# Block 2's keys and values as two split units, compression in four column groups of the array, and these units in another order

## The reference

```python
h = rms_norm(x, norm_mix_g[i]);  proj = h @ w_in[i]
q_r, k_r, v_r, g_r, q_n, kv_n, gate_n, m_a, m_b = jnp.split(proj, cuts, axis=-1)
y_ret = (silu(g_r) * groupnorm(retention(rotary(q_r), rotary(k_r), v_r))) @ w_o_ret[i]
kv = kv_n.reshape(B, T, 6, NSA_KV_GROUPS, NSA_HD)      # k_c v_c k_s v_s k_w v_w, 2 groups of 64
kc = compress(k_c)  # blocks of 32 tokens, every 16: gelu((block + pos) flattened to 2048 @ w1) @ w2
vc = compress(v_c)
o_n = g0 * softmax(q kc) vc + g1 * softmax(q k_s) v_s + g2 * softmax(q k_w) v_w   # 16 heads of 64
y_nsa = o_n @ w_o_nsa[i]
x = x + (sigmoid(m_a) * y_ret + sigmoid(m_b) * y_nsa) @ w_out[i]
h = rms_norm(x, norm_ffn_g[i]);  a, b = split(h @ w_ffn_in[i]);  x = x + (silu(a) * b) @ w_ffn_out[i]
```

## Time and profile before

| what | value |
|---|---|
| median of 3 runs | 2225.61 us (2225.45 to 2229.24) |
| the profiled execution | 2225.84 us |
| its span in the trace | 2224.0 us |
| TensorE busy | 2128.4 us, 96% of the span |
| TensorE weight loads busy | 1881.1 us, 85% |
| VectorE busy | 846.8 us, 38% |
| ScalarE busy | 1057.9 us, 48% |
| GpSimd busy | 1604.9 us, 72% |
| weights read | 336.83 MB |

### The profile page before, as it was taken

How to read it: one execution, slowest core, us unless ns; L and a number is a source line. 1 busy time by engine, 2 the same in 40 slices (tenths; PEclk the granted TensorE clock), 3 DMA queues, 4 the chain that set the end, 5 groups by cost and what they waited for, 6 DMA issues and landing times. The chain is left out here.

```text
span 2224.0 us, 33226 instructions
## 1 busy us (share of the span) xinstructions
PE 2128.4 (96%) x13056; PEld 1881.1 (85%) x13056; DVE 846.8 (38%) x1849; ACT 1057.9 (48%) x2037; POOL 1604.9 (72%) x1279
## 2 busy tenths in 40 slices
PE   7999999996999999999999999999999999999998
PEld 6788999795878999897687888998987777889996
DVE  3432464166532465091402182331433220553221
ACT  3344565443244565444452475444454522665443
POOL 6295898892386898898892508988997844348887
PEclk9899999997999999999999999999999998999999
DMA  7644455451044575545345404554554445225553
GB/s 246 130 157 146 152 190 190 174 201 38 1 151 152 163 232 191 201 161 180 114 180 186 152 1 152 178 176 178 183 180 149 152 155 173 76 69 165 185 190 123
DMA packets 217696, 343.17 MB, mean 154 GB/s; under 512 B 8611, under 2 KB 124419, under 8 KB 217413
## 3 DMA queue, kind: packets, MB, share of 16 engines
q1 hardware_dynamic: 205688, 331.35, 43.3%
q10 hardware_dynamic: 11853, 9.70, 2.3%
HBM read 336.83 MB, written 4.19 MB: 153 GB/s over the span
## 5 line engine op out<-in xcount | busy, mean ns | idle before, releaser
L1354 POOL TENSOR_TENSOR w_lo<-ring,w_hi 128x512 fp32r<-128x512 f32 x1184 | 1544.8, 1322 | 519.8 <-ACT w_hi L1460 466.6
L1460 ACT ACTIVATE w_hi<-ring 128x512 fp32r<-128x512 f32 x1184 | 742.7, 633 | 839.2 <-PE bank L701 338.3
L701 PE MATMUL bank<-x_hi,w_hi 128*128 128x256 f32 x2080 | 593.9, 286 | 13.9 <-POOL w_lo L1354 13.6
L704 PE MATMUL bank<-x_lo,w_hi 128*128 128x256 f32 x2080 | 591.0, 284 | 0.0
L705 PE MATMUL bank<-x_hi,w_lo 128*128 128x256 f32 x2080 | 590.9, 284 | 0.0
L701 PEld LDWEIGHTS bank<-x_hi,w_hi 128*128 128x128 f32 x2080 | 401.8, 193 | 17.2 <-issue 9.9
L704 PEld LDWEIGHTS bank<-x_lo,w_hi 128*128 128x128 f32 x2080 | 402.0, 193 | 0.2
L705 PEld LDWEIGHTS bank<-x_hi,w_lo 128*128 128x128 f32 x2080 | 401.7, 193 | 0.0
L726 PE MATMUL bank<-w_hi,x_hi 128*128 128x512 f32 x720 | 292.7, 407 | 20.0 <-POOL w_lo L1354 16.5
L729 PE MATMUL bank<-w_lo,x_hi 128*128 128x512 f32 x720 | 283.9, 394 | 0.0
L730 PE MATMUL bank<-w_hi,x_lo 128*128 128x512 f32 x720 | 283.7, 394 | 0.0
(11 more groups left out here) (314 smaller groups left out, 2396.4 us busy)
## 6 DMA issues: line engine op xcount, KB each, us to landing
ring<-in_w_in SPq DMA_DIRECT2D x72, 1024.0 KB, 6.7
ring<-in_ffn_w_up SPq DMA_DIRECT2D x44, 1024.0 KB, 7.6
ring<-in_w_ffn_in SPq DMA_DIRECT2D x44, 1024.0 KB, 6.6
ring<-in_ffn_w_down SPq DMA_DIRECT2D x20, 1024.0 KB, 6.0
ring<-in_w_ffn_out SPq DMA_DIRECT2D x20, 1024.0 KB, 6.3
ring<-in_xattn_wkv SPq DMA_DIRECT2D x16, 1024.0 KB, 6.3
ring<-in_w_o_ret SPq DMA_DIRECT2D x16, 1024.0 KB, 6.0
ring<-in_od_w_in SPq DMA_DIRECT2D x12, 1024.0 KB, 7.0
```

Source lines behind the costliest of these rows:

```text
L701: m = mm(out_, view(w_hi)[:, k, :], x_hi[:, 4 * kh + k, :], start=start, stop=False)
L704: mm(out_, view(w_hi)[:, k, :], x_lo[:, 4 * kh + k, :], start=False, stop=False)
L1354: tt(view(w_lo), src, view(w_hi), ALU.subtract).then_inc(w_lo_ready, 1)
L1460: return A(o, i_, ACT.Copy, **kw)
```

## The change

The three units of keys and values become two split ones: `kk` (512 columns: the compression's keys and values, the selected keys, the window keys; by channels) and `vv` (304 columns: the selected and the window values and the gates; by tokens, with pieces of 304). Each loads two ranges of columns side by side into its slot. The order becomes `kk`, `qn0`, `cmp_k`, `qn1`, `cmp_v`, `mb0`, `vv`, `mb1`. The compression's 16 matmuls go in turn to four groups of 32 columns of the array, each with its own 32 partitions of bank 6; its four partial sums lie there one under the other, ACT copies them out, and one matmul with `c_fold` (four identity matrices of 32 one under the other) both adds and turns them; the Gelu then stands behind that. Turning the hidden layer and the product with the second matrix are put inside `mb0`, the scores with the compressed keys inside `vv`. The compressed values of two heads stand side by side, so L867's matmul serves two heads. VectorE zeroes the padded tensors in POOL's place, and `xnT` is no longer built in Block 2.

```diff
-            cols(units, f"{L}kv_a", w, KV_N, 384)
-            cols(units, f"{L}kv_b", w, KV_N + 384, 128)
-            cols(units, f"{L}kv_c", w, KV_N + 512, 304)
-            for j, n in enumerate("kv"):
...
+            two_ranges(f"{L}kk", 512, (0, KV_N, 384), (384, KV_N + 512, 128))
+            cols(units, f"{L}qn0", w, Q_N, 512)
+            compression("k")
+            cols(units, f"{L}qn1", w, Q_N + 512, 512)
+            compression("v")
+            cols(units, f"{L}mb0", w, M_B, 512)
+            two_ranges(f"{L}vv", VALUES, (0, KV_N + 384, 128), (128, KV_N + 640, 176))
+            cols(units, f"{L}mb1", w, M_B + 512, 512)
...
-                                    o_last=(a % 4 == 3 and b == 1), extra=a if b == 0 else None))
+                                    o_last=(a % 4 == 3 and b == 1), extra=a if a % 2 == 0 and b == 0 else None))
...
-                    mm(bank[b][:, c:c + SEQ], n_vc[:, a % 4, g, 64 - 64 * par:192 - 64 * par], n_pcT[:, a // 4, :],
-                       start=first, stop=False)
+                    mm(bank[b][:, c:c + SEQ], n_vc[:, a % 4 // 2, a // 8, :], n_pcT[:, a // 4, :], start=first, stop=False)
...
-                        m = mm(bank[6][0:2 * N_CMP, 0:256], n_x[j][:, lp, :], ring[:, s, lp * 256:(lp + 1) * 256],
-                               start=lp == 0, stop=lp == 15)
+                        part = 32 * (lp % 4)
+                        m = mm(bank[6][part:part + 32, 0:256], n_x[j][:, lp, :], ring[:, s, lp * 256:(lp + 1) * 256],
+                               start=lp < 4, stop=lp >= 12)
...
+                            m = mm(bank[7][:, (2 * j + c) * 32:(2 * j + c + 1) * 32], n_hid[j][:, c * P:(c + 1) * P], c_fold, start=True, stop=True)
...
+                hidden_units(0)
                 channel_major(f"{L}qn1", x_parts)
...
+                hidden_units(1)
+                token_major(f"{L}mb0", x_parts, second_half=turn_hidden, after=compressed)
+                token_major(f"{L}vv", x_parts, second_half=compressed_scores)
+                token_major(f"{L}mb1", x_parts)
...
-                for v in (n_ks, n_kw):
-                    nc.gpsimd.memset(v.rearrange("p a b -> p (a b)"), 0.0)
...
+                B.wait_full(dve, (f"{L}oret", 1, 1))
+                for v in (n_ks, n_kw):
+                    nc.vector.memset(v.rearrange("p a b -> p (a b)"), 0.0)
```

More of the change, by code:

```diff
@@ L353, in build @@
         rt_lo, rt_hi = parts[:, 0:16, :], parts[:, 16:32, :]
[L354 to L355 removed]
+        n_x = [E[:, 2 + j, :].rearrange("p (l c) -> p l c", l=16) for j in range(2)]
+        n_hid = [E[:, j, 0:256] for j in range(2)]
         g_hi, g_lo = f_hi, f_lo
@@ L1192, in _ @@
                 rows_projection(f"{L}oret", 4, rt_hi, rt_lo, 16, ready)
[L1193 to L1201 removed]
+                channel_major(f"{L}kk", x_parts)
@@ L1206, in _ @@
                     m.then_inc(full[6], 1)
                     unit_done()
-                    if j == 0:
-                        channel_major(f"{L}qn0", x_parts)
-                for j in range(2):
-                    B.wait_emptied(pe, ("hid", L, j))
-                B.take(pe, ("hidT", L), 7)
-                for j in range(2):
-                    for c in range(2):
-                        m = tr(bank[7][:, (2 * j + c) * 30:(2 * j + c + 1) * 30], n_hid[j][:, c * P:(c + 1) * P], ident[0:30, 0:30])
@@ new lines, in compressed @@
+                def compressed():
+                    B.wait_emptied(pe, ("hidT", L))
+                    pe.wait_ge(layer_loads, i * 32 + 32)
+                    B.take(pe, ("kc", L), 4)
+                    for c in range(2):
+                        m = mm(bank[4][0:NSA_HD, 0:30], n_w2[:, 0, c, :], n_hT[:, 0, c, 0:30], start=c == 0, stop=c == 1)
+                    m.then_inc(full[4], 1)
+                    B.take(pe, ("vc", L), 5)
+                    for g in range(2):
+                        for c in range(2):
+                            m = mm(bank[5][0:N_CMP, g * NSA_HD:(g + 1) * NSA_HD], n_hT[:, 1, c, g * N_CMP:(g + 1) * N_CMP], n_w2[:, 1, c, :],
+                                   start=c == 0, stop=c == 1)
+                    m.then_inc(full[5], 1)
@@ new lines, in compressed_scores @@
+                def compressed_scores():
+                    B.wait_emptied(pe, ("kc", L))
+                    for j in range(2):
+                        for q in range(2):
+                            B.wait_emptied(pe, (f"{L}qn{j}", q))
+                    B.take(pe, ("cs", L), 6)
+                    for t in range(TT):
+                        for a in range(NSA_HEADS):
+                            m = mm(bank[6][:, (t * NSA_HEADS + a) * N_CMP:(t * NSA_HEADS + a + 1) * N_CMP],
+                                   n_qT[:, a // 2, t * P:(t + 1) * P], n_kc[:, 2 * (a // 8) + a % 2, 0:N_CMP], start=True, stop=True)
+                    m.then_inc(full[6], 1)
@@ L1252, in _ @@
                 B.wait_emptied(pe, ("vc", L))
-                for k in (f"{L}kv_b", f"{L}kv_c"):
-                    for t in range(TT):
-                        B.wait_emptied(pe, (k, "t", t))
-                B.wait_emptied(pe, (f"{L}kv_a", 1))
-                B.wait_emptied(pe, (f"{L}kv_c", 0))
+                for t in range(TT):
+                    B.wait_emptied(pe, (f"{L}vv", "t", t))
+                B.wait_emptied(pe, (f"{L}kk", 1))
                 heads(nsa_heads(i))
```

169 lines of the change are left out of this document (81 added, 88 removed).

## The result

| kernel | median of the runs | span of the profiled execution | ratio to the kernel before |
|---|---|---|---|
| before | 2226.20 us (2225.45 to 2229.24, 4 runs) | 2224.0 us | |
| after | 2205.77 us (2202.04 to 2209.41, 4 runs) | 2207.5 us | 0.9906 (0.9886 to 0.9925) |

Faster by 0.94%, some 20.4 us between the medians; 2200 was predicted. Of the difference between these two profiles, 4.6 us arose ahead of the changed code: the last matmul of `oret` in the first pass starts at 1173.98 here and at 1169.38 in the trace before. So I compare stretches, not ends.

The account below looks back on a forecast made before the run. TensorE, busy 96% of the span, was taken as the bound, with the ring's round trip deciding its waits. 2225.8 - 18.4 (stretches) - 6.9 (heads) = 2200.5, said as 2200 us; 65% for 2195 to 2207, 8 in 10 for 2188 to 2210.

Parts of the forecast that it names:

- The ring sets the pace, and the faster compression buys nothing: Block 2's two-slot weight ring: compression at 1.8 instead of 7.07 us buys almost nothing, TensorE waiting 4.8 us at `qn1`.
- The round trip of 10.1 us: Weight ring: time from a freed slot to TensorE's first matmul of the unit loaded into it, read at `qn0`.
- `qn1` at +30.1 us, `mb0` at +49.3: Block 2, each pass: starts of these two units on TensorE, in us after the end of `oret`.
- The clock: TensorE behind the waits: 1.7 us lost to the low clock, charged once a pass at `mb0`, vanishing at `qn1`.
- each wait costs more clock: Rival, waits at `qn1` and `mb0`: longer low clock and delayed POOL cost some 4 us more a pass, 2208 us; 15%.
- Scores 10.9 us at a low clock, ACT 1.4 us: Inside and after `vv`: scores take 10.9 us at low clock; ACT's longer list loses 0.7 us at each of two places.
- Stretch 96.2 us a pass: TensorE from the end of `oret` to the turn of `pcT`: 96.2 us against a mean of 105.4, saving 18.4 in two passes.
- The narrow piece, 0.14 us a matmul: `vv`, the 304-column token unit: 0.14 us a matmul, six to a piece, 0.84 us a piece, 6.7 us a unit.
- Part 1: TensorE work of the units: 23.0 us removed and 18.1 added, net 4.9 us less a pass.
- Heads 6.9 us: Heads: 32 matmuls with `n_vc` become 16, each saving 0.43 us, 6.9 us in all, down to 5 if VectorE shows through.
- Zeroing at nothing: VectorE's zeroing of 5,184 columns, at most 6.7 us, costs no time; its work fills about 16 of 23.2 us available.
- the 25.3 us that were booked: Whole kernel: the forecast savings, 18.4 us in the two stretches of Block 2 and 6.9 us in the heads.

Follow-up runs that it names:

- e1: The changed kernel with all 16 compression matmuls in one column group instead of four: 2203.28 us, ratio 0.9887 to the kernel before.
- e6: The kernel before the change with only the four column groups added, partial sums not added up: 2230.52 us, ratio 1.0016 to the kernel before.
- e3: The changed kernel with the compression matrices loaded into tensors of their own instead of ring slots: 2174.39 us, ratio 0.9758 to the kernel before.
- e5: The e3 kernel with the compression in one column group again: 2196.87 us, ratio 0.9861 to the kernel before.
- e7: The changed kernel with VectorE's gating products cut to 8 columns and its additions to 16: 2201.84 us, ratio 0.9887 to the kernel before.
- e2: The changed kernel with 20 matmuls of 512 columns, results unused, behind each compression: 2200.03 us, ratio 0.9872 to the kernel before.
- c0_after: The changed kernel itself, unedited, run again as the yardstick: 2204.35 us, ratio 0.9893 to the kernel before.
- e9_after_unpaired: The changed kernel with the paired compressed values undone, one `n_vc` matmul for each of 16 heads: 2207.92 us, ratio 0.9909 to the kernel before.

## Why the prediction came out

The time lies in the forecast's 2195 to 2207 us, and the order of events was right too. By its steps:

- **The ring sets the pace, and the faster compression buys nothing.** Shown from four sides: taking the groups away costs nothing (e1), adding them to the old program costs 3.5 us (e6), taking the compression's two units a pass out of the ring gives 30 us (e3), and there the groups give 22.5 (e5).
- **The round trip of 10.1 us**: 10.26 at `qn1` and 11.29 at `mb0` in the first pass, 9.7 and 10.4 in the second, and 10.0 for both in e7's first pass. What differs is the time from the request to ACT's first rounding, 8.1 us at `qn1` and 9.2 at `mb0` in the first pass; why isn't settled.
- **`qn1` at +30.1 us, `mb0` at +49.3**: measured +31.4 and +53.6 in the first pass, +30.9 and +51.3 in the second (after the end of `oret` as in the earlier trace rows). This is the step that was off, as a size. In the first pass the 4.3 us are: `qn0`'s slot free at 21.2 instead of 20.0, as POOL's lead was 2.26 and not 3.15 us (VectorE held it up, e7); 0.2 of round trip; the slot of `qn1` free 10.9 us after its start, not 9.1; and 1.2 us of the longer load. In the second pass the slot of `qn0` is free as late, but the round trips are shorter and `qn1` gives up its slot 10.0 us after its start.
- **The clock, "charged once, at `mb0`; at `qn1` it vanishes"**: wrong for `qn1`. The slow start doesn't vanish in the wait behind it, since POOL's pieces wait for ACT, and ACT's for TensorE's starts: the 1.29 us of idle time ahead of POOL's sixth remainder in the rows above are this. It lets go of the slot 1.8 us later, and the load of `mb0` starts later by as much. The rival "each wait costs more clock" had this, at some 4 us a pass on top of the 1.7 charged; e2 measures 4.6 and 3.3 us for both up to the scores, and 2.2 to 2.7 a pass at the end.
- **Scores 10.9 us at a low clock, ACT 1.4 us**: 9.3 and 9.4 us at a granted clock of 0.76 and 0.75, as the low clock came only after a part of them; ACT 0.6. From `mb0` to the turn it is 45.7 us where 46.9 were forecast, and this took back 1.2 of the 3 us.
- **Stretch 96.2 us a pass**: 99.3 and 97.0. 14.5 us were gained, not 18.4.
- **The narrow piece, 0.14 us a matmul**: starts 0.41 us apart for three, 0.137. (The 1.37 us of a wide piece in Part 1 are 23.72 - 1.8 divided by the 16 pieces; the 8 that stands in that sum is a slip, and the result is right.)
- **Heads 6.9 us**: 5.6 here, 6.0 and 6.25 in the experiments. The distance between matmuls was right; by the matmul of the last pair a pass is 3.0 us ahead, seven times 0.43, and the eighth gains nothing (5.2 us from there to `onsa`, as before). In the first pass `onsa` also waits 1.60 us for the input of VectorE where it had waited 0.91 for POOL.
- **Zeroing at nothing**: nothing, but for a smaller cushion than I said. The compression's input was ready at 1194.3, 3.4 us before TensorE asked for it; by my 16 of 23.2 us it would have been 7:

```profile
1178.96 0.91 DVE L2432 MEMSET region<- 128x1024 f32 x1 [0.16 <-issue]
...
1185.95 5.14 DVE L2450 TENSOR_TENSOR E<-bank,R_b 64x120 f32<-64x120 f32 x16
1191.19 1.38 DVE L2457 TENSOR_TENSOR E<-E,vecs 128x480 f32<-128x480 f32 x1
...
1194.20 0.09 DVE L2458 MEMSET E<- 128x32 f32 x1
```

The memsets cost 0.91 us for 1,024 columns, less than assumed; the two-input instructions cost twice and more what they did before (gating 6.01 us for four instead of 2.6; additions 1.4 to 1.7 each instead of 0.62).

Of the 25.3 us that were booked, the rows show 20.1: the stretches had 3.9 us too much and the heads 1.3, so nothing cancels between these two, and the 0.3 us that the medians show beyond 20.1 are within the variation. What is luck lies inside the stretch: `mb0` came 3.1 us late in the mean, and the scores and ACT, booked too dear, gave 1.2 of it back.

## What to carry to other kernels

Before making work on the bound engine faster, ask when the unit behind it can be there: with two slots, it comes one round trip (request, load, first rounding, first remainder) after the release of the unit two before it, and all that is saved in between is given back as a wait, and once more as a low clock behind the wait. Units with little work for TensorE are dear in such a ring, as each holds a slot for the time of a whole load; taken out of it, they gave more here than the change itself. And see what else stands in the queue of the engine that makes the intermediate result: in the old order the Gelu stood behind roundings that waited for a load.

## What was not expected of the hardware

- VectorE and GpSimd hold each other up when both read two tensors from SBUF. A gating product of 512 columns took 0.63 us when POOL had no remainders to write and 1.5 us beside them; a remainder took 1.28 us alone, 1.30 beside memsets and 1.66 beside the gating. The Trainium skill (SBUF — State Buffer, SBUF: two separate sides) says that a VectorE instruction with two inputs in SBUF contends with a GpSimd instruction that reads SBUF, and that the one that starts first has the shared ports for the whole instruction while the other waits. The trace agrees that they contend, down to the product of 8 columns that takes 0.75 us; memsets, with no input, left POOL nearly alone. It doesn't show that one always waits for the whole of the other: by an estimate from these rows, the 6.0 us of the four products hold 2.5 us of gating and 4.6 of remainders at their undisturbed lengths, 7.1 in all, so a part of them ran at the same time.
- Ahead of the first changed instruction two executions were 4.6 us apart; one wait of Block 1, for VectorE, was 8.1 us long in the one and 5.6 in the other, the rest lies in small pieces. The stretches of Block 2 differed by up to 2.4 us a pass between executions of nearly the same code (c0_after and e9_after_unpaired). What is smaller than that needs many runs, or rows in place.
